# Differential attention: VectorE takes the maximum of the next unit's scores before it joins the two parts of the unit at hand

## The reference, cut to what matters

```
s = concatenate([einsum('bhmqd,bhmkd->bhmqk', qr, kr),
                 einsum('bhmqd,bhmkd->bhmqk', qp, kc)], axis=-1) * scale
p = softmax(s, axis=-1)
w = p[:, :, 0] - lam * p[:, :, 1]
o = einsum('bhqk,bhkd->bhqd', w, v)
```

## Time and profile before

| | us |
|---|---|
| median of 3 runs | 2365.26 |
| lowest and highest | 2364.72, 2370.28 |
| the profiled execution's own time | 2369.64 |
| span of that execution's trace | 2367.8 |
| TensorE busy in the span | 2222.2 (94%) |
| VectorE busy | 1168.0 (49%) |
| ScalarE busy | 514.5 (22%) |
| mean granted TensorE clock | 0.972 |

### The profile page before, as it was taken

One profiled execution on the slowest core, in us unless ns is written; L12 is line 12 of the kernel. 1 busy time (PEld: TensorE's weight loads), 2 busy tenths in 40 slices (PEclk: granted clock), 3 DMA queues, 4 the chain that ended last, 5 costly groups with the idle time before them and its releaser, 6 DMA issues.

```text
span 2367.8 us, 39712 instructions
## 1 busy us (share of the span) xinstructions
PE 2222.2 (94%) x17498; PEld 1749.6 (74%) x17498; DVE 1168.0 (49%) x2177; ACT 514.5 (22%) x1086; POOL 157.4 (7%) x180
## 2 busy tenths in 40 slices
PE   6999779997989999898999999999999999999998
PEld 3444578885478887776565666889988877788998
DVE  1364543444065554554545545278542353227884
ACT  3233532221010000000434434100002133302200
POOL 0003011221000000000111211100000000000000
PEclk8999889999999999999999999999999899999999
DMA  7122012111112235452212212334445422233443
GB/s 293 72 71 71 18 38 74 74 74 38 53 72 89 89 116 207 178 196 72 72 71 71 89 54 74 122 143 170 162 140 197 158 91 90 72 127 140 167 172 125
DMA packets 38100, 260.65 MB, mean 110 GB/s; under 512 B 4631, under 2 KB 6183, under 8 KB 7336
## 3 DMA queue, kind: packets, MB, share of 16 engines
q1 hardware_dynamic: 34416, 248.83, 29.0%
q10 hardware_dynamic: 2616, 6.11, 0.7%
q0 software_dynamic: 896, 3.18, 0.4%
HBM read 256.49 MB, written 1.08 MB: 109 GB/s over the span
## 4 chain that ended last, share of the span: by engine, by line
PE 50%; DVE 1%; ACT 0%; issue 0%; DVEq 0%; ACTq 0%
PE pairs L302 14%; PE pairs L1557 10%; PE pairs L180 10%; PE pairs L2498 4%; PE bank L302 3%; PE pairs L1686 1%; PE pairs L2452 1%; PE bank L1595 1%; PE bank L1660 1%; PE bank L2432 1%; PE bank L1650 1%; PE bank L1625 1%; PE bank L513 0%; PE bank L1634 0%; PE bank L2408 0%; PE bank L1652 0%
## 5 line engine op out<-in xcount | busy, mean ns | idle before, releaser
L180 PE MATMUL pairs<-h_sb,ring_sb 128*128 128x512 f32 (+1 forms) x1008 | 345.2, 503 | 13.4 <-DVE h_sb L1525 6.0
L180 PEld LDWEIGHTS pairs<-h_sb,ring_sb 128*128 128x128 f32 x1008 | 194.7, 194 | 162.6 <-issue 140.3
L1557 PE MATMUL pairs<-h_sb,ring_sb 128*128 128x512 f32 (+1 forms) x784 | 264.8, 493 | 6.8 <-ACT h_sb L546 6.8
L1557 PEld LDWEIGHTS pairs<-h_sb,ring_sb 128*128 128x128 f32 x784 | 147.5, 191 | 113.7 <-issue 103.0
L302 PE MATMUL pairs<-mid 128*128 128x128 f32 (+1 forms) x1232 | 182.0, 303 | 0.0
L302 PEld LDWEIGHTS pairs<-mid 128*128 128x128 f32 x1232 | 166.7, 193 | 8.4 <-issue 0.2
L322 DVE TENSOR_TENSOR mid<-ring_sb 128x512 f32<-128x512 f32 (+1 forms) x98 | 66.9, 682 | 155.4 <-DMA ring_sb<-weights 96.6
L180 PE MATMUL pairs<-big,ring_sb 128*128 128x256 f32 (+1 forms) x576 | 121.7, 376 | 3.4 <-DVE one L2622 2.8
L302 PE MATMUL pairs<-h_sb,ring_sb 128*128 128x128 f32 (+1 forms) x736 | 109.4, 304 | 14.9 <-ACT h_sb L546 11.2
L180 PEld LDWEIGHTS pairs<-big,ring_sb 128*128 128x128 f32 x576 | 108.3, 211 | 16.5 <-DVE one L2622 3.2
L302 PEld LDWEIGHTS pairs<-h_sb,ring_sb 128*128 128x128 f32 x736 | 99.1, 198 | 21.7 <-issue 16.4
(11 more groups left out here) (462 smaller groups left out, 3506.8 us busy)
## 6 DMA issues: line engine op xcount, KB each, us to landing
ring_sb<-weights SPq DMA_DIRECT2D x237, 1024.0 KB, 4.8
x_sb<-tokens ACTq DMA_DIRECT2D x1, 2048.0 KB, 12.2
mid<-bias_table POOLq DMA_DIRECT2D x1, 1536.0 KB, 7.9
const_table<-consts ACTq DMA_DIRECT2D x1, 1410.0 KB, 7.1
mid<-bias_table POOLq DMA_DIRECT2D x1, 1024.0 KB, 12.9
out<-x_sb ACTq DMA_DIRECT2D x4, 256.0 KB, 2.2
lora_w<-lora ACTq DMA_DIRECT2D x1, 512.0 KB, 15.6
vec_table<-vectors SPq DMA_DIRECT2D x1, 285.0 KB, 22.1
```

The costliest lines, as they stand in the source:

```text
L180: last = pe.matmul(out, w[:, k, c, :], rhs(j * kt + k), start=(j == 0 and k == 0), stop=(j * kt + k == k_end - 1))
L1557: ins = pe.matmul(m.pairs[:, at % 2, c, 0:T], w[:, k, c, :], m.h[:, k, TOK - T:TOK], start=(k == 0), stop=(k == 7))
```

## The change

In `diff_dve` the block that takes max(t) moves from behind join(t-1) to ahead of it. No instruction, wait or operand changes, and the other engines' programs are the same as before. The two blocks:

```
     for t in range(n + 1):
+        if t < n:
+            keys = units[t][2]
+            dve.wait_ge(sem["scores"], t + 1)
+            if t >= 2:
+                dve.wait_ge(sem["exps"], t - 1)
+            dve.tensor_reduce(m.row_max[:, 2 * (t % 2):2 * (t % 2) + 2], m.bank[:, 2 * (t % 2):2 * (t % 2) + 2, 0:keys],
+                              AX.X, ALU.max, negate=True).then_inc(sem["row_max"], s.one("row_max"))
         v = t - 1
         if 0 <= v < n:
...
             dve.scalar_tensor_tensor(p[:, 0, 0:keys], p[:, 1, 0:keys], share, p[:, 0, 0:keys], ALU.mult, ALU.add) \
                 .then_inc(sem["parts_joined"], s.one("parts_joined"))
-        if t < n:
-            keys = units[t][2]
-            dve.wait_ge(sem["scores"], t + 1)
-            if t >= 2:
-                dve.wait_ge(sem["exps"], t - 1)
-            dve.tensor_reduce(m.row_max[:, 2 * (t % 2):2 * (t % 2) + 2], m.bank[:, 2 * (t % 2):2 * (t % 2) + 2, 0:keys],
-                              AX.X, ALU.max, negate=True).then_inc(sem["row_max"], s.one("row_max"))
```

## The result

| | before | with the change |
|---|---|---|
| median, us | 2367.10 (4 runs, 2364.72 to 2370.28) | 2396.02 (4 runs, 2395.39 to 2397.84) |
| profiled execution, span | 2367.8 | 2394.0 |
| first join to last join | 50.3 | 78.8 |
| mean granted TensorE clock | 0.972 | 0.961 |

The ratio is 1.0122, with a 95% interval of 1.0106 to 1.0138: the change makes the kernel 28.9 us slower.

What follows compares the result with a forecast made beforehand. It took a VectorE-ScalarE ring with TensorE waiting as the bound, replaced by one through TensorE; 37.1 + 39.3 + 1.5 = 77.9 us against 50.3, so +27.6 and 2393 us, range 2377 to 2399.

Steps and rivals of the forecast that it cites:

- The new ring: Attention stage: join(t-1), turn(t-1), weighted(t-2), scores(t+1), max(t+1), prelude, join(t) in a row; 5.15 to 7.37 us per 512-key unit.
- Steps 1 to 8: First eight join-to-join steps, 256 keys with 512-key scores and max in 7 and 8; low clock, 37.1 us.
- Steps 9 to 14: Join-to-join steps of the 512-key units, the first mixed; two thirds low and one third full clock, 39.3 us.
- one third at full clock: Chosen share for steps 9 to 14, between low 43.6 and full 30.6 us; all low would give +31.9.
- Step 15: Last join-to-join step, no max ahead of the join any more; 1.48 us against 3.85, the one place of gain.
- The busy shares: TensorE busy 47% of a 256-key turn at full clock, 61% at low; taken as grounds for the low clock.
- a rise throughout the 256-key units: Case of the clock rising during the 256-key units; said to take off up to another 9.4 us.
- step 9: Mixed step, turn with 512 keys and weighted with 256; 4.82 us at full clock, 6.71 at low.
- From the scan on the trace is the same, only later: Sign for the part behind the attention stage: nothing changes there except that it starts later.
- full clock throughout: Rival for the attention stage: the ring is as forecast but the clock holds; +9.1, 2374 us; chance 0.13.
- The rival of a gain: Rival for the attention stage: scores done before the join, so the ring opens; -14 us, 2351; chance 0.03.
- The absorbed loss: Rival: the scan behind the stage hides the delay, wholly or mostly; chance 0.04, half of it within 0.3%.

Runs made afterwards that it cites:

- weighted_last: The changed kernel with TensorE's weighted products moved one iteration later, behind the next scores, so its list reads turn(t-1), scores(t+1), weighted(t-2); 2376.03 us.
- scores_first: The changed kernel with TensorE issuing scores one unit earlier, ahead of turn(t-1) and weighted(t-2); 2348.31 us, ratio 0.9909 to before.
- after_filled: The changed kernel with extra, overwritten products on TensorE while it waits for the join, 5 per 256-key and 8 per 512-key unit; 2373.30 us.
- TensorE's half: The kernel before the change with only TensorE's list reordered, scores one unit earlier, and VectorE's list as before; 2366.63 us, ratio 0.9988.
- before_filled: The kernel before the change with extra, overwritten products in TensorE's gaps, 3 per 256-key and 4 per 512-key unit; 2364.14 us, ratio 0.9971.

## Why the prediction was right

It said 2393 (2377 to 2399), 27.6 us more than the median of 2365.26 that it had; the measured median is 2396.02, 28.9 us more than the 2367.10 beside it (25 to 33 by the ratio's interval). By its own steps:

- The new ring (join, turn, weighted, scores, max, join) is what the timelines show, step by step, without slack. Shown by the trace, and by weighted_last and scores_first, which shorten and open it.
- The price of a step at either clock. Forecast 4.42 us for 256 keys at the low clock, measured 4.34; 7.37 us for 512 keys, measured 7.27; at full clock 3.24 and 5.15, measured 3.15 (256.74 to 259.89 in the timeline of after_filled) and 5.05. The estimate is 0.1 us too long throughout: from the start of the maximum to the start of the join it is 1.05 and 1.58 us, where the sum had 1.13 and 1.67, because the reciprocals start a little before the end of the maximum's row.
- Steps 1 to 8: forecast 37.1 us, all at the low clock; measured 36.5 (251.90 to 288.39), with the clock at 0.54 from 250 to 286. Right in the level; the 0.6 us are the 0.1 us a step.
- Steps 9 to 14: forecast 39.3 us with one third at full clock; measured 40.7 (288.39 to 329.11) at 0.60, which is nearer to a fifth. The one third was a choice and not read from any row, and the sum of these steps came out 1.4 us too low. That the clock would rise behind some bursts and fall again is what happened, but the share could have been another: the rows of before give the price at the two levels, but not the share.
- Step 15: forecast 1.48 us, measured 1.60 (329.11 to 330.71), against 3.85 before. This is the one gain of the change, as said.
- Sum: 77.9 against 78.8, so +27.6 forecast and +28.5 measured in the stage. The agreement within 1 us is in part luck, as the steps that were priced too long and the share of full clock that was put too high work against each other.
- The busy shares by which the low clock was argued for steps 1 to 8 have not been tested as its cause. weighted_last, where TensorE was busy 16.40 of 20 us at 0.50, and the kernel before, where it was busy 8.77 of 14 us at 1.00, speak against a reading by the share alone. That filling the waits brings the full clock back is shown.
- Two slips change nothing in the forecast: a rise throughout the 256-key units would take off 9.8 us (37.1 less 27.4), not 9.4, and step 9 at the low clock adds up to 6.72, not 6.71.
- "From the scan on the trace is the same, only later" held roughly, not exactly. From the last join to the end of the span it is 2063.3 us, 4.1 less than before (2067.4), and ahead of the stage there are 1.8 us more (L973 starts at 246.57 instead of 244.81). The code is the same in both places, and these are single executions, where the runs of the kernel before alone reach from 2364.72 to 2373.97 us. One difference that can be seen is the clock: before, it was 0.62 and 0.97 in the 20 and the following 40 us behind the last join; with the change:

```profile
330.70:350.70 20.00, 12.60 (x187) 11.90 (x186) 7.04 (x16) 7.66 (x16) 1.39 (x2) 0.74 0.00 1
350.70:390.70 40.00, 36.03 (x1083) 33.69 (x1080) 18.02 (x48) 10.67 (x29) 11.84 (x18) 1.00 0.15 56
```

- Of the rivals, full clock throughout (+9.1 forecast) was realised in after_filled, where the joins took 7.9 us more. The rival of a gain, which said -14 us if scores ran ahead, was realised in scores_first with -21 (by the medians), of which the joins show 18.2 (50.3 to 32.1). The forecast fell short mostly in the 256-key units, priced at a gain of 0.5 us each; there the steps fell from about 2.6 us to 1.8 (257.53 to 259.32 in its timeline).
- The absorbed loss did not happen: 28.5 us in the stage, 28.9 in the medians.

The reasoning from order rather than from waits was what mattered. In the waits of before, nothing hints at a cost: VectorE waited 1.8 us for scores in the whole stage. The cost shows when the lists of two engines are laid side by side and followed around.

## What to carry to other kernels

Where an instruction is moved ahead on an in-order engine, follow what it waits for back through the other engines' lists. If that leads to the same instruction that it has overtaken, for an earlier unit, a new ring is closed, and all the work on the way is on the path: max(t+1) overtook join(t), and its scores stand behind join(t-1). It is worth trying to move the stages of a software pipeline by the same number of units on every engine; VectorE's half cost 29 us, TensorE's half gained 3, and both together gained 21. When a change opens gaps on TensorE, price its work at both clock levels: here the ring cost 8 us at full clock, and the low clock another 21.

## What the runs showed of the hardware

In the changed kernel the granted clock read 0.50 for 33 us (253 to 286) while TensorE was busy for 20.99 of them, with gaps of at most 2.17 us. With small products put into the gaps (after_filled) it read 1.00 from 247 to 309 us, a net gain of some 23 us for work that is thrown away. Such filler helped even the kernel before, by 6.9 us, of which the stage shows 2.9. How much of the time TensorE is busy did not tell the level by itself: weighted_last had 0.50 at 16.40 of 20 us busy.

What stays open is that nearly the same code, from the last join to the end, took between 2059 us (before_filled) and 2067 us (before) in these profiles. The clock behind the stage differs between them (0.62 to 0.83 in the first 20 us). Single executions differ by as much: the 18 runs of before beside before_filled reach from 2364.74 to 2373.97 us, and the profiled execution of before_filled, 2360.62 us, is itself 3.5 us below its median. Whether the filler causes any of the rest was not tried.
